# Four changes of order in a two-block transformer kernel: copies and a chunk split in the first attention, the residual's tiles, two norm starts, and the bias loads

## What is computed

```python
def first_block(x, ...):
    for i in range(2):
        h = rmsnorm(x, norm_mix[i])
        x = x + (forgetting_attention(h, ...) if i == 0 else retention(h, ...))
        h = rmsnorm(x, norm_ffn[i])
        x = x + swiglu(h, ffn_w_in[i], ffn_w_out[i])
    return rmsnorm(x, final_norm)

def forgetting_attention(h, w_in, b_f, w_out):      # 8 heads of 128, blocks of 128 queries
    s = einsum(q, k) * scale + (c_query - c_key)     # c: running sum of log-sigmoid gates
    p = softmax(where(query >= key, s, -inf))
    return (p @ v) @ w_out

def second_block(x, rel_bias_table, ...):
    for i in range(2):
        u = rmsnorm_2(x, norm_pre[i])
        y = nsa_mixer(u, ...) if i == 0 else diff_mixer(u, ...)
        x = x + rmsnorm_2(y, norm_post[i])
    return x

def nsa_mixer(u, table, w_in, ...):                  # 16 heads of 64, in 4 groups
    q, kc, vc, ks, vs, kw, vw, gate, z = split(u @ w_in)
    k_cmp, v_cmp = compress(kc, ...), compress(vc, ...)   # blocks through a small MLP
    # attention to compressed blocks, to selected blocks and to a window,
    # each with a bias by lag from the table; gated and summed
```

## Time and profile before

| what | value |
|---|---|
| time, median of 3 runs | 2096.8 us (2096.77 to 2097.56) |
| the profiled execution's own time | 2095.72 us |
| its span | 2094.4 us |
| TensorE busy | 2045.0 us (98%) |
| VectorE, ScalarE, GpSimd busy | 965.7, 776.6, 336.5 us (46%, 37%, 16%) |
| read from HBM | 181.33 MB, 89 GB/s over the span |

### The profile page before, as it was taken

The page is one execution under the profiler, slowest core; times in us unless marked ns, Lnnn a source line. Parts: engine busy times, 40 slices in busy tenths (PEclk is TensorE's granted clock), DMA queues, the critical chain, the costliest instruction groups (busy, mean ns, idle before and its releaser), DMA issues.

```text
span 2094.4 us, 26714 instructions
## 1 busy us (share of the span) xinstructions
PE 2045.0 (98%) x10149; PEld 1658.6 (79%) x10149; DVE 965.7 (46%) x1968; ACT 776.6 (37%) x1548; POOL 336.5 (16%) x501
## 2 busy tenths in 40 slices
PE   7998999999999999999999999999998999999998
PEld 5887888888888886788888888887787888777766
DVE  4438334443354344435533443364435664535445
ACT  4226332222233222333322222242336884435453
POOL 2103100000002120000110000044003764312211
PEclk9999999999999999999999999999998999999999
DMA  5330143332324331132243333325321102323212
GB/s 177 101 101 11 61 124 95 98 96 87 109 64 148 101 91 50 51 100 92 69 133 101 91 100 95 96 83 175 100 71 61 30 24 101 108 76 109 67 48 81
DMA packets 96766, 187.32 MB, mean 89 GB/s; under 512 B 8407, under 2 KB 16639, under 8 KB 96512
## 3 DMA queue, kind: packets, MB, share of 16 engines
q1 hardware_dynamic: 90288, 164.35, 25.9%
q0 software_dynamic: 6352, 21.27, 3.2%
HBM read 181.33 MB, written 4.26 MB: 89 GB/s over the span
## 4 chain that ended last, share of the span: by engine, by line
PE 87%; ACT 5%; DVE 3%; issue 2%; POOL 1%; DMA 1%; SPq 0%; ACTq 0%; DVEq 0%; POOLq 0%
PE bank L754 61%; PE bank L790 8%; PE bank L1265 5%; PE bank L1024 2%; PE bank L1186 1%; PE bank L1163 1%; PE bank L1279 1%; ACT sc L1795 1%; PE bank L1009 1%; PE bank L1095 1%; DVE wl L1966 1%; PE bank L1302 1%; ACT xn L1789 1%; DMA raw<-in_nsa_w_in 1%; PE bank L1152 1%
## 5 line engine op out<-in xcount | busy, mean ns | idle before, releaser
L1966 DVE TENSOR_TENSOR wl<-raw,wh 128x1024 fp32r<-128x1024 f32 x306 | 375.1, 1231 | 779.3 <-ACT wh L1382 778.6
L1382 ACT ACTIVATE wh<-raw 128x1024 fp32r<-128x1024 f32 x306 | 321.0, 1053 | 841.6 <-PE bank L754 783.5
L754 PE MATMUL bank<-hTh,wh 128*128 128x512 f32 (+2 forms) x1200 | 468.1, 390 | 3.4 <-ACT kvc L1723 3.2
L754 PE MATMUL bank<-hTl,wh 128*128 128x512 f32 (+2 forms) x1200 | 467.4, 390 | 0.0
L754 PE MATMUL bank<-hTh,wl 128*128 128x512 f32 (+2 forms) x1200 | 467.3, 389 | 0.0
L754 PEld LDWEIGHTS bank<-hTh,wh 128*128 128x128 f32 (+2 forms) x1200 | 224.4, 187 | 51.9 <-ACT kvc L1723 3.3
L754 PEld LDWEIGHTS bank<-hTh,wl 128*128 128x128 f32 (+2 forms) x1200 | 224.2, 187 | 48.3
L754 PEld LDWEIGHTS bank<-hTl,wh 128*128 128x128 f32 (+2 forms) x1200 | 224.4, 187 | 48.0
L754 PE MATMUL bank<-wh,hTh 128*128 128x512 f32 x400 | 156.5, 391 | 0.1
L754 PE MATMUL bank<-wh,hTl 128*128 128x512 f32 x400 | 155.7, 389 | 0.0
L754 PE MATMUL bank<-wl,hTh 128*128 128x512 f32 x400 | 155.6, 389 | 0.0
(11 more groups left out here) (383 smaller groups left out, 3117.0 us busy)
## 6 DMA issues: line engine op xcount, KB each, us to landing
raw<-in_ffn_w_in SPq DMA_DIRECT2D x88, 512.0 KB, 3.6
raw<-in_ret_w_in SPq DMA_DIRECT2D x48, 512.0 KB, 3.8
raw<-in_ffn_w_out SPq DMA_DIRECT2D x44, 512.0 KB, 3.7
raw<-in_diff_w_in SPq DMA_DIRECT2D x32, 512.0 KB, 3.7
raw<-in_fox_w_in SPq DMA_DIRECT2D x24, 512.0 KB, 4.0
raw<-in_nsa_w_in SPq DMA_DIRECT2D x20, 512.0 KB, 3.6
raw<-in_ret_w_out SPq DMA_DIRECT2D x16, 512.0 KB, 3.7
raw<-in_fox_w_out SPq DMA_DIRECT2D x8, 512.0 KB, 3.7
```

What stands on the lines that cost most here:

```text
L754: i = pe.do.matmul(dst, x, y, start=first and k == 0 and q == 0, stop=stop)
L1382: act.do.activation(M.hl[n % HL_SLOTS][0][:, 0:m], M.raw[n % RAW_SLOTS][:, 0:m], ACT.Copy).then_inc(*T.up("act_hi", n))
L1966: dve.do.tensor_tensor(wl[:, 0:m], M.raw[n % RAW_SLOTS][:, 0:m], wh[:, 0:m].bitcast(F32), ALU.subtract).then_inc(*T.up("dve_lo", n))
```

## The change

1. In the fox attention ScalarE's loop does the copy of tile n-4 ahead of the exponential of tile n. One split of a chunk, the last before the attention on both engines, moves into the attention, behind step 8.
2. ScalarE makes the residual's four tiles, three behind the turn of tile 2 and one behind that of tile 3 (which moves from `act_nsa` into `act_final`); GpSimd's four instructions go. `pool_x` becomes `act_x`.
3. GpSimd loads the first four bias tiles behind the second half of the compression weights.
4. Where `sums=True`, `dve_by_tile` no longer releases the two held splits at its end; `dve_ffn` releases them behind the turn of tile 3.

```diff
@@ pool_program
-    for t in range(4):
-        pool.wait_ge(*at("dve_gained", t))
-        pool.wait_ge(*at("act_sum", ("fin", t, 1)))
-        pool.do.tensor_scalar(M.X[:, t, :], M.gained[t], M.norm["fin"][2][:, t, 6:7], None, ALU.mult).then_inc(*up("pool_x", t))
@@ pool_nsa
-    for h in range(4):
-        load_bt(h)
...
     load_w1("k")
     pool.wait_ge(*at("pe_cmp", ("hidden", 0)))
     load_w1("v")
+    for h in range(4):
+        load_bt(h)
@@ act_fox
-    act_product(act, T, M, 4)
+    act_product(act, T, M, 3)
     T.note("act", "fox heads")
...
     for n in range(32 + 6):
+        if 0 <= n - 4 < 32:
+            turned_out(n - 4)
         if n < 32:
             exp(n)
-        if 0 <= n - 4 < 32:
-            turned_out(n - 4)
         if 0 <= n - 6 < 32:
             after(n - 6)
+        if n == 8:
+            act_split(act, T, M)
@@ act_final
+    def residual(t):
+        act.wait_ge(*T.at("act_sum", ("fin", t, 1)))
+        act.wait_ge(*T.at("dve_gained", t))
+        act.wait_ge(*T.at("pool_cell", ("fin", t, "o")))
+        act.do.activation(M.X[:, t, :], M.gained[t], ACT.Copy, scale=M.norm["fin"][2][:, t, 6:7]).then_inc(*T.up("act_x", t))
...
     act_turn(act, T, M, "n4", 2)
+    residual(0)
+    residual(1)
+    residual(2)
+    act_turn(act, T, M, "n4", 3)
+    residual(3)
@@ act_nsa
-    act_by_tile(act, T, M, late=("n4", {0: (3,)}))
+    act_by_tile(act, T, M)
@@ dve_by_tile
-    while dve.held:
+    while dve.held and not sums:
         dve_release(dve, T, M)
@@ dve_fox
-    dve_product(dve, T, M, 4, 4, take_v(1))
+    for _ in range(3):
+        dve_split(dve, T, M)
+    for o in range(4):
+        take_v(1)(o)
...
+        if n == 8:
+            dve_split(dve, T, M)
@@ dve_ffn
     for t in late[1]:
         dve_turn(dve, T, M, late[0], t)
+    while dve.held:
+        dve_release(dve, T, M)
     dve_split(dve, T, M)
```

## The result

The changed kernel takes **2083.4 us** (median of 4 runs, 2083.23 to 2085.87) where the kernel before takes 2096.8 (4 runs, 2096.28 to 2097.56): a ratio of 0.994, 95% interval 0.9928 to 0.9952, 13.3 us less. Five further runs of the same kernel, reported with the experiments, gave 2083.0 (0.9934, 0.9922 to 0.9947). The profiled execution is the slowest of the four: 2085.87, span 2084.6, mean granted clock 0.995, where the other three have 0.997.

What follows compares the result with a forecast made beforehand. TensorE, busy 98% of the span, bounds the kernel, so only its waits can go: -2.5 (first attention) - 2.9 (feed-forward starts) - 4.6 (NSA start) = -10.0 us, from 2096.8 to 2086.8 us; range 2083.8 to 2092.0.

Steps and rivals of the forecast that it cites:

- The attention, -2.5: First (fox) attention: earlier copies and the moved split together save 2.5 us, bounds +0.4 and -5.0.
- Six heads at 0.26 and 1.3 of TensorE's trail: First attention: early copies save 0.26 us in each of six heads, and TensorE trails VectorE by 1.3 us less.
- The exchange of the split, +0.4: First attention: moving the split behind step 8 gains 1.6 us at the start, loses 2.05 there: 0.4 us lost.
- VectorE keeps the pace: First attention: VectorE, whose work isn't cut, sets the pace of a head, so the gain lies mid-bounds at -2.5 us.
- rival 3: First attention: TensorE becomes the bound and all 5.0 us of its waits go, 2084.3 us; chance 0.04.
- The feed-forwards, -2.9: Starts of both feed-forwards: two splits behind `hTl` remove TensorE's waits of 1.42 and 1.51 us whole.
- The NSA start, -4.6: Start of the NSA heads: TensorE's 3.2 us wait for `kvc` goes, plus 1.4 us lost to the lowered clock.
- rival 1: NSA start: the load stays late behind GpSimd's transfers, so -4.6 is lost, 2091.4 us; chance 0.12.
- rival 2: First attention gives nothing because VectorE's wait at the split grows: +0.4 in place of -2.5, 2089.7 us; chance 0.12.
- rival 5: First attention: copies waiting for TensorE's turn hold up exponentials, 13.3 us lost, 2102.6 us; chance 0.03.
- rival 6: At all the places: the waits return as others right behind and nothing moves, 2096.8 us; chance 0.06.
- rival 4: First attention: the moved split meets GpSimd's pair of `Lc` fills and stands for them, +3.4, 2090.2 us; chance 0.03.

Runs made afterwards that it cites:

- experiment 1: Kernel before with only ScalarE's copy of tile n-4 put ahead of exponential n in the first attention: 2092.3 against 2096.9 us (0.9979).
- experiment 6: Changed kernel with the split put back ahead of the first attention: 2085.6 us against 2096.4 of the kernel before (0.9947).
- experiment 4: Kernel before with only the residual's four tiles moved from GpSimd to ScalarE: 2090.7 against 2096.9 us (0.9972).
- experiment 8: Changed kernel with the first attention's split behind step 20 and `hTl` a step later: 2082.6 us against 2096.4 of the kernel before (0.9935).
- experiment 5: Kernel before with only the four bias tiles loaded later, behind the value half of the compression weights: 2090.9 against 2096.4 us (0.9974).

## Why the prediction was right, term by term

The direction came as forecast, and so did the three places and the cause of the wait at each. The gain did not: it is 13.3 us where 10.0 was forecast, 0.4 us more than the range allows.

**The attention, -2.5, was too small: -3.94.** The working had three parts. Six heads at 0.26 and 1.3 of TensorE's trail, 2.9 together, are what experiment 1 shows part by part; but it measures 4.07, since the step "Each of six heads then saves 0.26 us" left out that the heads also move against GpSimd's fills. From the first maximum to the sixth `hTl` the kernel of experiment 1 is 2.70 us shorter than before: 1.63 in the waits for `hTh`, 0.82 in two pairs of casts, 0.32 in idle times too short to be listed and 0.1 in the rest, less 0.2 that weighings give back, more of which now stand beside a fill. That the casts stood clear of the fills was not aimed at: this 0.8 is luck. The exchange of the split, +0.4, measured +0.74 alone and +0.16 beside the copies: right in sign, and of a size that a measurement can't tell from nothing. So all of the attention's gain is the copies'. "VectorE keeps the pace" was the argument against rival 3, and it holds for part of the stage only: in the changed kernel TensorE has no listed wait from 175 us on, and in experiments 1 and 6, without the split in the loop, none from 164.

**The feed-forwards, -2.9, measured -3.34**, whole, and the splits that now come late cost nothing. The term was short by what a printed wait leaves out, 0.2 us each. At the NSA start that happens to be within the 1.4 counted for the clock.

**The NSA start, -4.6, measured -4.65**, but the working gave the change too little credit. It took both edits to be needed for its 3.7 us of margin. One is enough, the residual tiles by 0.9 us and the bias tiles by more.

**The NSA attention was not in the sum, and the traces show no gain there.** It is +1.42 in the profiled execution and +0.15 in the next trace. Ten traces have the same order in it. Of nine of them those whose granted clock is at 0.50 (1.2 GHz) for 10 to 14 us in all near the start take 499.2 to 499.5 us, and those where it is low for 17 take 500.6 to 500.8; the tenth, experiment 4's, has a second low stretch, shown in the last section. One wait did grow with the residual's move: the second at this start is 1.26 us in the traces with ScalarE's tiles and unchanged order there (the changed kernel's two and experiments 4, 6 and 8) and 0.98 in those without. No row shows why.

**What is left, 1.4 us, stays open.** The medians differ by 13.3, the stages that the change touches by 11.9. With the 1.4 that the attention and the 0.4 that the feed-forwards gave beyond their terms the forecast would be 2085.0, inside the range; the open 1.4 us put the time below it. The clock is one candidate. Of the 58 runs of the kernel before that were timed beside the experiments 44 have a mean granted clock of 0.995, 4 have 0.994 and 10 have 0.996, and eight of the nine of the changed kernel have 0.997. A difference of 0.002 is 4.2 us of 2090, give or take 2 by the rounding; 1.7 of it had gone behind the `kvc` wait (0.69, 0.50 and 0.96 in three windows of 2 us from 1452) and are in the -4.65 already. But a higher mean clock is not by itself a shorter time: in experiment 5 the four runs at 0.997 took 2090.2 to 2091.8 us and the three at 0.995 took 2090.8 to 2091.0. The start, which scatters by 1.5 us, is another candidate. So is the first attention: in the traces of experiments 4 and 5 the clock also fell for 3 to 4 us from about 161, behind the wait of 1.07 that the changed kernel no longer has, and the stretch is 0.35 us longer than in that of before. No run separates the three. In the runs of single edits 0.997 is common only where the wait for `kvc` is gone: 5 of 7 and 4 of 7 for experiments 4 and 5, 1 of 10 for experiment 1. But 4 of 5 in experiment 6 have 0.995 without that wait. What decides the length of the low clock stays open.

**Rivals.** 1, 2, 5 and 6 did not come; 3 came in part, 3.94 of its 5.0 us. 4 named the right pair: the split met no fill (GpSimd's ended at 167.2, the split began at 168.6).

## What to carry to other kernels

When two engines feed a third in a loop, put first what is ready first: a copy whose source lies there for a microsecond costs nothing ahead of an instruction that still waits; behind it, it cost 0.26 us per head here and 1.4 at the end. Work that must be done somewhere, like a split of 2 us on two engines, cost about as much inside a busy loop as ahead of it, in both attentions; look for idle time of both engines before moving it. And test each of two edits that remove one wait alone: here either was enough.

## What the runs showed of the hardware

**VectorE and GpSimd slow each other.** Kernel before, VectorE then GpSimd, the pair of casts of step 25 and the pair of fills that overlaps it, and for comparison the casts of step 21, which begin 0.2 us after the fill ahead of them has ended:

```profile
189.19 0.85 DVE L2148 CAST Rc<-ident 8x512 fp32r<-8x512 f32 x2
...
195.80 1.27 DVE L2148 CAST Rc<-ident 8x512 fp32r<-8x512 f32 x2
...
185.94 3.05 POOL L537 TENSOR_SCALAR Lc<-ident 8x512 fp32r<-8x512 f32 x2 [3.69 <-PE bank L898]
192.96 3.39 POOL L537 TENSOR_SCALAR Lc<-ident 8x512 fp32r<-8x512 f32 x2 [3.97 <-PE bank L898]
```

VectorE loses 0.42 us and GpSimd 0.34. The casts are not alone in it. Of the kernel before again, a weighing beside the fill that runs from 172.38 to 175.43, which takes 0.42 us where no fill runs:

```profile
173.99 0.78 DVE L2176 TENSOR_SCALAR tr<-tr,smalls 128x384 f32<-128x384 f32 x1
```

So a pair of casts that comes clear of a fill saves 0.42 us only if no weighing takes its place. The Trainium skill (SBUF — State Buffer, Terms) says that the two engines arbitrate for one port pair and that the loser is blocked; that they get into each other's way the trace bears out, that one stands for the other's whole instruction (1.5 us a fill) it does not. Likewise VectorE's scaling of a tile took 2.13 us at 1415.26 beside GpSimd's residual tile and 1.28 without it.

**The clock after one and the same wait differs.** Beside the two traces above: behind TensorE's wait of 1.45 us at about 1965 the clock is 1.00 in the kernel before. In experiment 4 the same wait has 0.88 and 0.78 in the two windows of 5 us around it, and it takes 65.73 us from there to the next wait where before took 64.08. A time from one profiled execution of this kernel can't be read closer than 2 us; its stages ahead of the second attention can.
